# A decoder layer on one Trainium2 core: the norm weight spread by TensorE, and the inverse root entering the turn of x as a diagonal matrix

## What is computed

```python
def rms_norm(x, w):
    xf = x.astype(jnp.float32)
    y = xf * lax.rsqrt(jnp.mean(xf * xf, axis=-1, keepdims=True) + EPS) * w.astype(jnp.float32)
    return y.astype(x.dtype)
...
h = rms_norm(x, norm_w[l])
proj = jnp.einsum("btd,dc->btc", h, w_in[l])       # 2048 x 12304: q, k, v, z, gates of both branches
...                                                # gated delta rule (8 heads), block attention (8 heads)
merged = jax.nn.sigmoid(g_gdn) * y_gdn + jax.nn.sigmoid(g_moba) * y_moba
x = x + jnp.einsum("btd,de->bte", merged, w_o[l])
```

## Time and profile before

| what | value |
| --- | --- |
| median of 3 runs | 1591.86 us |
| lowest and highest of them | 1590.28 and 1592.87 us |
| the profiled execution | 1592.19 us |
| its span, first to last instruction | 1590.5 us |
| mean granted TensorE clock | 0.999 |
| TensorE busy | 1563.0 us (98%) |
| VectorE, ScalarE, GpSimd busy | 1077.0, 790.6, 197.5 us |

### The profile page before, as it was taken

The page is one execution under the profiler, slowest core; times in us unless marked ns, Lnnn a source line. Parts: engine busy times, 40 slices in busy tenths (PEclk is TensorE's granted clock), DMA queues, the critical chain, the costliest instruction groups (busy, mean ns, idle before and its releaser), DMA issues. The chain is left out here.

```text
span 1590.5 us, 20663 instructions
## 1 busy us (share of the span) xinstructions
PE 1563.0 (98%) x7739; PEld 1297.3 (82%) x7739; DVE 1077.0 (68%) x1317; ACT 790.6 (50%) x1049; POOL 197.5 (12%) x181
## 2 busy tenths in 40 slices
PE   6999999999999999999999999999999989999999
PEld 6888888888888888888888888888888878887787
DVE  6655745745646646555558778867677999878864
ACT  5434534444445444445444347556564855555542
POOL 4202002002002002011021011010110111102020
PEclk9999999999999999999999999999999999999999
DMA  8314315224224224233234348676657778878883
GB/s 269 92 29 126 80 36 151 53 70 115 57 81 125 59 66 112 59 86 92 59 94 124 114 145 239 199 193 230 146 175 195 225 218 240 242 225 174 224 179 60
DMA packets 198048, 217.04 MB, mean 136 GB/s; under 512 B 7843, under 2 KB 140198, under 8 KB 196902
## 3 DMA queue, kind: packets, MB, share of 16 engines
q1 hardware_dynamic: 177030, 162.73, 34.5%
q0 software_dynamic: 20960, 53.52, 14.6%
HBM read 191.03 MB, written 29.39 MB: 139 GB/s over the span
## 5 line engine op out<-in xcount | busy, mean ns | idle before, releaser
L822 PE MATMUL bank<-h_hi_r,w_hi 128*128 128x512 f32 x1008 | 414.5, 411 | 0.0
L826 PE MATMUL bank<-h_hi_r,w_raw_r 128*128 128x512 f32 x1008 | 395.0, 392 | 0.0
L824 PE MATMUL bank<-h_lo_r,w_hi 128*128 128x512 f32 x1008 | 393.4, 390 | 0.0
L2255 DVE TENSOR_TENSOR ring_lo<-operands,ring_hi 128x1024 fp32r<-128x1024 f32 x224 | 271.7, 1222 | 117.1 <-ACT ring_hi L1629 116.2
L1629 ACT ACTIVATE ring_hi<-operands 128x1024 fp32r<-128x1024 f32 x224 | 235.8, 1062 | 217.7 <-PE bank L1269 159.6
L826 PEld LDWEIGHTS bank<-h_hi_r,w_raw_r 128*128 128x128 f32 x1008 | 189.1, 188 | 42.0
L822 PEld LDWEIGHTS bank<-h_hi_r,w_hi 128*128 128x128 f32 x1008 | 189.7, 188 | 38.0 <-issue 1.7
L824 PEld LDWEIGHTS bank<-h_lo_r,w_hi 128*128 128x128 f32 x1008 | 189.9, 188 | 37.2 <-issue 1.7
L1265 PE MATMUL bank<-ring_hi,h_hi_r 128*128 128x512 f32 x480 | 190.9, 398 | 5.5 <-issue 5.5
L1267 PE MATMUL bank<-ring_lo,h_hi_r 128*128 128x512 f32 x480 | 189.2, 394 | 0.0
L1786 DVE TENSOR_TENSOR w_raw_r<-w_raw,w_hi 128x2048 fp32r<-128x2048 f32 x64 | 147.8, 2310 | 37.1 <-ACT w_hi L1325 36.1
(11 more groups left out here) (323 smaller groups left out, 2158.9 us busy)
## 6 DMA issues: line engine op xcount, KB each, us to landing
w_raw<-in_w_in_dram SPq DMA_DIRECT2D x64, 1024.0 KB, 6.1
operands<-in_w_in_dram SPq DMA_DIRECT2D x64, 512.0 KB, 4.6
operands<-in_w_o_dram SPq DMA_DIRECT2D x32, 512.0 KB, 5.0
operands<-in_w_in_dram POOLq DMA_DIRECT2D x16, 512.0 KB, 7.9
gates<-e_block POOLq DMA_DIRECT2D x16, 512.0 KB, 5.6
operands<-in_w_out_gdn_dram SPq DMA_DIRECT2D x16, 512.0 KB, 4.9
operands<-gates SPq DMA_DIRECT2D x16, 512.0 KB, 6.2
operands<-in_w_out_moba_dram SPq DMA_DIRECT2D x16, 512.0 KB, 5.4
```

The source lines that it names most:

```text
L822: pe.matmul(PJ[slot % 2][:], w_hi[slot % 2][:, c], h_hi[:, k, :], start=(k == 0), stop=False, skip_group_check=True)
L824: pe.matmul(PJ[slot % 2][:], w_hi[slot % 2][:, c], h_lo[:, k, :], start=False, stop=False, skip_group_check=True)
L826: mm = pe.matmul(PJ[slot % 2][:], w_lo[slot][:, c], h_hi[:, k, :], start=False, stop=(k == KT - 1), skip_group_check=True)
L2255: dve.tensor_tensor(ring_lo[:, n % RINGS, :], operand(q, p, j), ring_hi[:, n % RINGS, :].bitcast(F32), ALU.subtract).then_inc(s["op_lo"], 1)
```

## The change

The 1 MB load of `nw` is taken out. In its place the 2048 weights are loaded as 16 rows of 128 (`nw16`, 8 KB, in a corner of `sg`), ahead of tile 0 of x. TensorE spreads them: 16 products, each with a column of the identity (step 0, so 128 times the same) and `nw16`, which puts one row on all partitions, into the four banks of the turns. VectorE copies the banks into `nw`, four times 128 x 512, the last quarter first.

The scaling is divided. x times `nw` no longer needs the inverse root: `x_weigh(t)` on VectorE (1536 columns) and one instruction of GpSimd (512 columns) write to a new buffer `xw` with room for two tiles. From tile 2 on both wait until the turn of two tiles before has ended. `x_diag(t)` on VectorE multiplies the identity by `rsx`, which gives a diagonal matrix (128 x 128, in a corner of `mgt`, two of them). The turn is now a product of `xw` and this diagonal: `out[c, t] = sum over s of xw[s, c] * diag[s, t]`, which turns the block and scales each token at once. It is an ordinary float32 product instead of a transpose.

```diff
--- before.py
+++ after.py
@@ -183,6 +183,7 @@
 LEVELS = (4, 8, 16, 32, 64)
 NL = len(LEVELS)
 PAIRED = P // 2
+NW_SET = 2 * NL - 1 + 4
 
 (HC_G, HC_CG, HC_B, HC_NB, HC_NBE, HC_KD, HC_GL) = range(7)
 NHC = 7
@@ -272,6 +273,8 @@
         ab = mgt[:, 1, P:P + NT * 2 * H].rearrange("p (t c) -> p t c", t=NT)
         ba = mgt[:, 0, :6 * NT * H].rearrange("p (b t h) -> p b t h", b=6, t=NT)
         alog, dtb = mgt[:, 1, 0:H], mgt[:, 1, H:2 * H]
+        nw16 = sg[:KT, 0, 0, 0:P]
+        diag = mgt[:, 0, 2 * P:4 * P].rearrange("p (i c) -> p i c", i=2)
         ssx, rsx = mgt[:, 1, 2 * H:2 * H + NT], mgt[:, 1, 2 * H + NT:2 * H + 2 * NT]
 
 
@@ -289,6 +292,7 @@
         xt = sb("x_tiles", [P, NT, D], at=tmp)
         nw = sb("norm_w_rows", [P, D], at=tmp)
         xsq = sb("x_square", [P, D], at=tmp)
+        xw = sb("x_weighted", [P, 2, D], at=tmp)
         tmp.close()
 
         rawc, rawc_r = {}, {}
@@ -499,8 +503,8 @@
                 sp.dma_start(xt[:, t, :], xs[t * P:(t + 1) * P, :]).then_inc(x_loaded[t], 16)
 
             sp.dma_start(ident[:], consts[:, C_ID, :]).then_inc(s["ident_loaded"], 16)
+            sp.dma_start(nw16, norm_w.rearrange("o (k p) -> (o k) p", p=P)).then_inc(s["nw_loaded"], 16)
             load_x(0)
-            sp.dma_start(nw[:], norm_w.broadcast_to([P, D])).then_inc(s["nw_loaded"], 16)
             load_x(1)
             load_x(2)
             sp.dma_start(w16[:], w_in3[:, :, COL_BETA:COL_BETA + 2 * H]).then_inc(s["w16_loaded"], 16)
@@ -673,13 +677,13 @@
             for tile, value in ((ones_f, 1.0), (eps, EPS), (lnscale, LNSCALE)):
                 pool.memset(tile[:], value).then_inc(s["sets"], 1)
 
-            pool.wait_ge(s["nw_loaded"], 16)
+            pool.wait_ge(s["masks"], NW_SET)
             for t in range(NT):
-                part = xt[:, t, X_SPLIT:]
-                pool.wait_ge(s["x_rstd"], 3 * t + 3)
-                pool.tensor_scalar(part, part, rsx[:, t:t + 1], None, ALU.mult).then_inc(s["x_scaled_b"], 1)
-                pool.wait_ge(s["x_scaled_b"], 2 * t + 1)
-                pool.tensor_tensor(part, part, nw[:, X_SPLIT:], ALU.mult).then_inc(s["x_scaled_b"], 1)
+                pool.wait_ge((s["x_loaded0"], s["x_loaded1"], s["x_loaded2"], s["x_loaded3"])[t], 16)
+                if t >= 2:
+                    pool.wait_ge(s["x_T"], 4 * (t - 1))
+                pool.tensor_tensor(xw[:, t % 2, X_SPLIT:], xt[:, t, X_SPLIT:], nw[:, X_SPLIT:], ALU.mult)\
+                    .then_inc(s["x_scaled_b"], 1)
             pool.wait_ge(s["ba_mm"], 1)
             for k in ("gk", "gq", "gv"):
                 pool.memset(rawc[k][:, 0:4], 0.0).then_inc(s["sets"], 1)
@@ -1182,15 +1186,24 @@
             pe.wait_ge(s["ident_loaded"], 16)
             xbank = (G0, G1, G2, A0)
 
+            pe.wait_ge(s["nw_loaded"], 16)
+            for k in range(KT):
+                mm = pe.matmul(xbank[k // 4][:, tile4(k % 4)], ident[:KT, k:k + 1].broadcast_to([KT, P]), nw16,
+                               start=True, stop=True)
+            mm.then_inc(s["rows_T"], 1)
+
             def x_turn(t):
                 for q in range(4):
                     g = 4 * t + q
                     if q in (0, 3):
-                        pe.wait_ge((s["x_scaled_a"], s["x_scaled_b"])[q // 3], (t + 1, 2 * t + 2)[q // 3])
+                        pe.wait_ge((s["x_scaled_a"], s["x_scaled_b"])[q // 3], (2 * t + 2, t + 1)[q // 3])
+                    if g == 0:
+                        pe.wait_ge(s["masks"], NW_SET)
                     if g >= 4:
                         pe.wait_ge(s["x_lo"], g - 3)
                     for k in range(4):
-                        mm = pe.transpose(xbank[q][:, tile4(k)], xt[:, t, (4 * q + k) * P:(4 * q + k + 1) * P], ident[:])
+                        mm = pe.matmul(xbank[q][:, tile4(k)], xw[:, t % 2, (4 * q + k) * P:(4 * q + k + 1) * P],
+                                       diag[:, t % 2, :], start=True, stop=True)
                     mm.then_inc(s["x_T"], 1)
 
             x_turn(0)
@@ -2145,13 +2158,24 @@
             last = H - 1
             level_masks()
             dve.wait_ge(s["masks"], 2 * NL - 1)
-            dve.wait_ge(s["nw_loaded"], 16)
-
-            def x_scale(t):
+            dve.wait_ge(s["rows_T"], 1)
+            for q in (3, 0, 1, 2):
+                dve.tensor_copy(nw[:, q * T:(q + 1) * T], (G0, G1, G2, A0)[q][:]).then_inc(s["masks"], 1)
+            dve.wait_ge(s["masks"], NW_SET)
+
+            def x_weigh(t):
+
+                dve.wait_ge((s["x_loaded0"], s["x_loaded1"], s["x_loaded2"], s["x_loaded3"])[t], 16)
+                if t >= 2:
+                    dve.wait_ge(s["x_T"], 4 * (t - 1))
+                dve.tensor_tensor(xw[:, t % 2, :X_SPLIT], xt[:, t, :X_SPLIT], nw[:, :X_SPLIT], ALU.mult)\
+                    .then_inc(s["x_scaled_a"], 1)
+
+            def x_diag(t):
 
                 dve.wait_ge(s["x_rstd"], 3 * t + 3)
-                dve.scalar_tensor_tensor(xt[:, t, :X_SPLIT], xt[:, t, :X_SPLIT], rsx[:, t:t + 1],
-                                         nw[:, :X_SPLIT], ALU.mult, ALU.mult).then_inc(s["x_scaled_a"], 1)
+                dve.tensor_scalar(diag[:, t % 2, :], ident[:], rsx[:, t:t + 1], None, ALU.mult)\
+                    .then_inc(s["x_scaled_a"], 1)
 
             def x_lo(t):
                 for q in range(4):
@@ -2160,17 +2184,21 @@
                                       h_hi[:, 4 * q:4 * q + 4, tile4(t)].bitcast(F32), ALU.subtract)\
                         .then_inc(s["x_lo"], 1)
 
-            x_scale(0)
-            x_scale(1)
+            x_weigh(0)
+            x_diag(0)
+            x_weigh(1)
+            x_diag(1)
             x_lo(0)
-            x_scale(2)
+            x_weigh(2)
+            x_diag(2)
             x_lo(1)
             dve.wait_ge(s["w16_hi"], 1)
             dve.tensor_tensor(w16s[:, :, 1, :], w16[:], w16s[:, :, 0, :].bitcast(F32), ALU.subtract).then_inc(s["w16_lo"], 1)
-            x_scale(3)
+            x_weigh(3)
+            x_diag(3)
             x_lo(2)
             split(0, 0)
-            dve.wait_ge(s["rows_T"], 1)
+            dve.wait_ge(s["rows_T"], 2)
             dve.tensor_copy(chan[:], A2[:, :P]).then_inc(s["rows_ready"], 1)
             x_lo(3)
             split(1, 1)
```

## The result

The changed kernel takes 1599.76 us (median of 4 runs, 1598.46 to 1600.76) against 1592.07 for the kernel before: ratio 1.0048, 95% interval 1.0036 to 1.0059. It is slower by 7.7 us, where +5.8 was forecast, and lies inside the range. The profiled execution took 1599.94, its span is 1597.9.

The account below looks back on a forecast made before the run. TensorE's stream bounds the kernel; its first stripe product is the yardstick. Tile 0's turn ending at 21.2, plus 4.5 and 10.7, gives 36.4 against 30.58: +5.8 on 1591.9 makes 1597.7 us, range 1593.3 to 1600.5.

Parts of the forecast that it names:

- What bounds the kernel: TensorE, busy 1563.0 of 1590.5 us: a shift of its unbroken stream's start moves the end by as much.
- The weight is not multiplied on arrival: Prologue: x arrived 5 us before the weight, ready at 12.05; the spread weight is 3.2 us later than the DMA's 8.8.
- The spreading: Sixteen fp32 products on TensorE from 3.5, clock rising 5.0 us in: end at 9.5, with 7.8 and 10.4 as ends.
- Copies 2.4, weighing 1.8, diagonal 1.25: VectorE ahead of tile 0's turn: four bank copies, 1536 columns weighed, diagonal 0.28 plus 0.98 held by GpSimd; turn starts 15.2.
- The remark in brackets: Tile 0's weighing: if GpSimd goes first, VectorE's weighing is held by as much as the diagonal otherwise, 0.98 us.
- The turn of tile 0: Sixteen fp32 products on TensorE from 15.2, clock rising 5.0 us in: 6.0 us, bounds 3.5 and 6.9, ending at 21.2.
- From tile 0 to tile 2, 4.5; from there 10.7: Tile 2's turn starts 4.5 us after tile 0's ends, before 6.2; then 10.7 to the first stripe product, before 9.6.
- Case A: Prologue as summed, with the clock low at the start of the first turn: +4 to +8 us, chance 0.6.
- Case B: TensorE's clock up sooner: 1.5 us of products raise it in spreading and first turn, +2.4 us (1594.3); chance 0.22.
- Case C: TensorE's clock stays low through the spreading and the first two turns: +10.0 us (1601.9), chance 0.1.
- Case D: VectorE's copies cost 1.1 instead of 2.4 and it does not collide with GpSimd: +3.5 us (1595.4), chance 0.06.
- "doubled turns": Experiments' rival theory: products in place of transposes cost 1.75 us each at the same clock, the rest hidden; no chance given.

Follow-up runs that it names:

- the first experiment: Weight spread by the 1 MB DMA again instead of TensorE, against the changed kernel, the rest unchanged; 1599.09 us, ratio 1.0046 to the kernel before.
- the second experiment: Against the changed kernel: old scaling and transposes restored, weight still spread by TensorE; 1595.93 us, ratio 1.0022 to the kernel before.
- second combined kernel: Changed kernel with 128-row spreading into own banks read by VectorE, ScalarE's diagonal, 4 fillers behind the spreading, none ahead; 1592.34 us, ratio 0.9997.
- (the first): Changed kernel with 128-row spreading into own banks read by VectorE, ScalarE's diagonal, 4 fillers ahead of the spreading, 8 behind; 1592.48 us, ratio 1.0000.

## Why the prediction was right, and where it was short

- **What bounds the kernel.** Right: the shift of the first stripe product, 7.5 us, went through 1550 us of stream to the end, 7.7.
- **The weight is not multiplied on arrival.** Right: x is there at 6.90, the weighing starts at 13.04 (12.05 forecast).
- **The spreading.** The step that failed: the end 9.5 was taken from a rise of the clock 5.0 us in, "nearest" to the unbroken work of rows 3. It was the other end, 10.4: there was no rise. The runs showed why the row was not near: it is of work over 128 rows, the spreading is over 16, and the clock stayed low under 16 rows wherever it was tried (7.2 and 12.7 us), while 128 rows in the same place saw it rise in 3.5. That is 0.9 us of the 1.7 that the forecast of the product (36.4) was short.
- **Copies 2.4, weighing 1.8, diagonal 1.25.** Measured 2.48, 1.76 and 1.28. The collision and its size were read rightly from the rows: held by 1.0. The profiles say more of how: GpSimd's multiply ends at 15.9 and the diagonal 0.1 behind it, and where GpSimd is ahead, VectorE's weighing ends 1.6 us behind the end of GpSimd's multiply each time (10.30 and 11.91 with the DMA's weight, 10.33 and 11.94 with ScalarE's diagonal too), though it takes 1.76 alone. So the later one waits for the end of the earlier. The Trainium skill ("SBUF — State Buffer", Who interferes with whom) has it so, a lock for the whole instruction, and this trace agrees. What was wrong is the 0.3 us more that the prediction drew from that rule: the multiply began its own 1.28 us while VectorE's weighing was ending, so the diagonal met only the rest of it. The remark in brackets, that it costs the same if GpSimd goes first, was half of it: in the first experiment it cost 2.1 in all, as the diagonal then meets the multiply of tile 1.
- **The turn of tile 0.** Forecast 6.0 with ends 3.5 and 6.9, measured 6.7 (16.05 to 22.8): the clock rose 6.1 us in, not 5.0. In other executions it rose 3.0 and 3.4 us in. That 6.0 came so near was luck within the bounds, since nothing in the rows fixed the rise; it is 0.7 of the 1.7. The last 0.1 lies in the stretches below. Filling the pause shows that it is the clock: 2.8 us less.
- **From tile 0 to tile 2, 4.5; from there 10.7.** Measured 4.4 and 10.9.
- **Rivals.** Case A, at the top of its own 4 to 8. Case B (rise after 1.5 us) is excluded by the spreading. Case C had the right spreading and the wrong turns. Case D is out, with copies of 2.48 us and a held diagonal. The "doubled turns" alone fall with the second experiment: half of the loss is there without them. The queue freed of 1 MB brought tile 1's squares from 11.36 to 9.56, which nothing used.

## What to carry to other kernels

An operand that gets earlier is worth what the last thing it is combined with allows: here the code weighs x without waiting for its root, but x had been there for 6 us when the weight came, and the 1 MB load that the spreading replaced had brought that weight 4 us earlier. Moving a load onto TensorE brings its whole tail with it: products at whatever clock the engine has there, copies out of the banks, and a pause behind them, in which the clock falls if it had risen. And before splitting work between VectorE and GpSimd look at what stands next in VectorE's order: the help can cost the short instruction behind more than it saves, here 1.0 us against 0.5.

## What the runs showed of the hardware

- Products over 16 rows did not raise TensorE's clock: 32 records in 7.16 or 7.17 us in the changed kernel and in every experiment with that spreading, and 12.7 us of them in a row with the 16-row fillers. The same number over 128 rows took 5.50, with the rise 3.5 us in.
- A pause of 5.6 us behind a risen clock let it fall (spreading over 128 rows); pauses of 0.2 to 1.0 us between turns did not (second combined kernel, all turns 3.81), nor did one of 1.3 (the first). In the kernel before with fillers it was down again behind two pauses, 1.18 and 2.18 us, with 4 transposes between them.
- GpSimd's multiply and VectorE's multiply of two operands from SBUF did not run beside each other: GpSimd's took 2.83 us behind VectorE's, and VectorE's of 1.76 took 2.86 behind GpSimd's. With one of VectorE's operands in a bank both kept their own 0.62 and 1.27 us.
- Transposes do raise TensorE's clock. In the second profile of the kernel before no ordinary product had run, and the first 12 transposes of tile 1 took 1.76 us, 0.135 apart on average with the waits for their banks, where 0.215 is the lower clock; tile 2's 16 took 3.22, most of them at the lower clock again. With the old scaling behind the spreading, 20 transposes took 3.56 us, where 4.5 would be the lower clock. In the first profile of before the first three turns took 3.65 us or more each. With 28 fillers ahead, 12 transposes stayed at 0.11. The Trainium skill, "TensorE: Matmul & The Clock Gate", Part 4: PE-mode transpose, has it that the clock does not engage for them; the trace differs, and it decides.
- The granted clock of a window reads 1.00 up to the first rise, though the spacing shows the lower clock. Windows of the kernel with 128 rows (columns as above), where the records from 3.3 to 6.8 are at the lower clock; the second window holds the fall in the pause, and there the column shows it:

```profile
0.00:10.00 10.00, 5.50 (x32) 5.34 (x32) 2.65 (x11) 4.72 (x8) 0.62 (x8) 1.00 0.74 275
10.00:20.00 10.00, 5.55 (x26) 5.55 (x27) 8.61 (x9) 3.29 (x7) 4.05 (x2) 0.68 1.03 275
```
